# A decoder trunk on one core: the down products of the last two feed-forward steps as one, inside the normalisation, and three of four query latent weight blocks prepared early

## What is computed

```python
def _swiglu(x, w_gate, w_up, w_down):
    return (jax.nn.silu(x @ w_gate) * (x @ w_up)) @ w_down

def _shared_latent(x, pos, wkv_a, kv_norm):
    kv = x @ wkv_a                                    # 1024 -> 256 + 64
    return _rms_norm(kv[..., :256], kv_norm), _rope(kv[..., 256:], pos)

# in each layer, h being the mixer's or the attention's output
x = _layer_norm(ALPHA * x + h, ln_g[l, 0], ln_b[l, 0])
x = _layer_norm(ALPHA * x + _swiglu(x, w_gate[l], w_up[l], w_down[l]), ln_g[l, 1], ln_b[l, 1])
# layer 1 begins with _shared_latent(x, ...) and _rms_norm(x @ wq_a, q_norm)     # 1024 -> 384
```

## Time and profile before

| | us |
|---|---|
| median of 3 runs (lowest, highest) | 2610.28 (2603.63, 2615.92) |
| the profiled execution's own time | 2611.03 |
| its span in the trace | 2609.2 |
| PE busy | 2415.3 |
| DVE busy | 1294.6 |
| ACT busy | 769.7 |
| POOL busy | 347.1 |

### The profile page before, as it was taken

The page is one execution under the profiler, slowest core; times in us unless marked ns, Lnnn a source line. Parts: engine busy times, 40 slices in busy tenths (PEclk is TensorE's granted clock), DMA queues, the critical chain, the costliest instruction groups (busy, mean ns, idle before and its releaser), DMA issues.

```text
span 2609.2 us, 35320 instructions
## 1 busy us (share of the span) xinstructions
PE 2415.3 (93%) x14022; PEld 2198.0 (84%) x14022; DVE 1294.6 (50%) x2467; ACT 769.7 (30%) x1469; POOL 347.1 (13%) x308
## 2 busy tenths in 40 slices
PE   7899999999999768999998888898999999999994
PEld 7799999999999667898987667687999989999993
DVE  4623433333333765677767778643234434433336
ACT  2331111111111233555546556412311111111112
POOL 2400000000000330000006545032000000000006
PEclk9899999999999888999999999899999999999997
DMA  4021111111111031000004444500211111101111
GB/s 158 26 65 49 49 48 35 29 48 48 48 49 41 20 121 44 18 14 5 11 21 158 155 152 152 179 25 25 65 49 49 34 49 49 50 30 36 49 41 65
DMA packets 137082, 153.99 MB, mean 59 GB/s; under 512 B 10256, under 2 KB 114224, under 8 KB 136808
## 3 DMA queue, kind: packets, MB, share of 16 engines
q1 hardware_dynamic: 124656, 110.07, 13.4%
q0 software_dynamic: 12288, 41.95, 5.1%
HBM read 142.24 MB, written 10.32 MB: 58 GB/s over the span
## 4 chain that ended last, share of the span: by engine, by line
PE 80%; DVE 9%; ACT 4%; issue 3%; POOL 2%; DMA 2%; SPq 0%; POOLq 0%; ACTq 0%; DVEq 0%
PE ps L214 23%; PE ps L216 22%; PE ps L215 22%; DVE split L207 4%; ACT split L202 2%; PE ps L2010 2%; PE ps L2045 2%; POOL plain L338 1%; POOL plain L340 1%; PE ps L2025 1%; PE ps L222 1%; PE ps L221 1%; PE ps L2026 1%; PE ps L2032 1%; PE ps L1555 1%
## 5 line engine op out<-in xcount | busy, mean ns | idle before, releaser
L214 PE MATMUL ps<-split 128*128 128x512 f32 (+6 forms) x3632 | 1244.5, 343 | 69.9 <-DVE split L207 23.6
L215 PE MATMUL ps<-split 128*128 128x512 f32 (+6 forms) x3632 | 1229.2, 338 | 0.0
L216 PE MATMUL ps<-split 128*128 128x512 f32 (+6 forms) x3632 | 1228.1, 338 | 0.0
L214 PEld LDWEIGHTS ps<-split 128*128 128x128 f32 x3632 | 694.5, 191 | 120.1 <-DVE split L207 28.9
L216 PEld LDWEIGHTS ps<-split 128*128 128x128 f32 x3632 | 694.8, 191 | 38.0
L215 PEld LDWEIGHTS ps<-split 128*128 128x128 f32 x3632 | 694.8, 191 | 37.1
L202 ACT ACTIVATE split<-plain 128x1024 fp32r<-128x1024 f32 (+8 forms) x446 | 313.3, 738 | 628.7 <-PE ps L222 406.1
L207 DVE TENSOR_TENSOR split<-plain,split 128x1024 fp32r<-128x1024 f32 (+7 forms) x422 | 355.7, 867 | 193.1 <-ACT split L202 190.2
L274 DVE TENSOR_TENSOR plain<-plain,ps 128x512 f32<-128x512 f32 (+2 forms) x396 | 268.6, 685 | 201.9 <-PE ps L216 196.6
L910 DVE TENSOR_TENSOR plain<-plain,ps 128x350 f32<-128x350 f32 (+1 forms) x132 | 68.1, 516 | 574.6 <-ACT plain L866 574.0
L207 DVE TENSOR_TENSOR split<-ps,split 128x512 fp32r<-128x512 f32 (+5 forms) x480 | 247.6, 555 | 153.9 <-ACT split L202 146.4
(11 more groups left out here) (145 smaller groups left out, 1427.1 us busy)
## 6 DMA issues: line engine op xcount, KB each, us to landing
plain<-w_gate SPq DMA_DIRECT2D x44, 512.0 KB, 4.7
plain<-w_up SPq DMA_DIRECT2D x44, 512.0 KB, 4.0
plain<-w_down SPq DMA_DIRECT2D x44, 512.0 KB, 4.4
plain<-x_prompt SPq DMA_DIRECT2D x8, 512.0 KB, 11.2
x_spill<-plain SPq DMA_DIRECT2D x1, 4096.0 KB, 18.6
plain<-wo SPq DMA_DIRECT2D x8, 512.0 KB, 4.9
plain<-x_spill SPq DMA_DIRECT2D x8, 512.0 KB, 7.7
y_prompt<-plain SPq DMA_DIRECT2D x8, 512.0 KB
```

The lines of the kernel that those rows point to most:

```text
L214: pe.matmul(out, still[0], moving[0], start=start, stop=False)
L215: pe.matmul(out, still[0], moving[1], start=False, stop=False)
L216: return pe.matmul(out, still[1], moving[0], start=False, stop=stop)
```

## The change

In both layers, step 10 does no down products of step 9 any more. The normalisation stage's units (`down_last`) sum four chunks, two of step 9 and two of step 10, so that there are ten groups of 18 units instead of eleven. A unit then is 12 matmuls, for the tail 8. The hidden parts of both parities are read; the last two blocks of w_down are split earlier, between the chunks of step 10, into slot 0 of the gate and up buffer (`split_down_last`, `wd_last`), which the first chunk of step 10 has left. PE waits for the hidden part per tile.

In layer 0, blocks 2 and 3 of wkv_a are split at step 9 of the normalisation stage instead of step 3, since block 2 lies where `k.wd` and the hidden parts were. Blocks 4, 5 and 6 of the latent weights are split at units 3, 5 and 7, and only block 7 at unit 9. SP's load of the tables stands behind the last block of wq_a instead of behind that of wkv_a. The places of the eight blocks are a list of offsets now.

```diff
--- before.py
+++ after.py
@@ -155,7 +155,8 @@
         every = {n: rows for n in ("stats", "root", "scale", "normed", "gained", "rows")}
         every.update({n: 2 * tiles + 1 for n in ("turned", "turned_hi", "turned_lo")})
         every.update(gain_in=32, norm_steps=7 * rows + 2, unit_done=2 * rows, unit_taken=2 * rows)
-        ffn = dict(every, unit_done=2 * rows * steps, unit_taken=2 * rows * steps, steps=2 * steps - 2, x_scaled=rows)
+        ffn = dict(every, unit_done=2 * rows * (steps - 1), unit_taken=2 * rows * (steps - 1), steps=2 * steps - 4,
+                   x_scaled=rows)
         ffn.update({"raw_in%d" % i: 2 * 16 * steps for i in range(3)})
         ffn.update({n: 6 * steps for n in ("w_hi", "w_lo")})
         ffn.update({n: 2 * PARTS * steps for n in ("gu_done", "silu", "h_mul")})
@@ -649,6 +650,7 @@
     def __init__(self, k, layer, nt):
         self.k, self.layer, self.nt, self.ph = k, layer, nt, "ffn%d" % layer
         self.steps = k.ff // (2 * P)
+        self.groups = self.steps - 1
         self.x_ph = ("mix", "att")[layer]
 
     def name(self, name):
@@ -752,8 +754,8 @@
 
     def latent_weights(self, eng, step, act):
 
-        if self.layer == 0 and step == 3:
-            for n in range(4):
+        if self.layer == 0 and step in (3, self.k.tiles + 1):
+            for n in ((0, 1) if step == 3 else (2, 3)):
                 latent_split(eng, self.k, n, act)
 
     def split_tile(self, eng, st, i, hi, lo, act):
@@ -771,6 +773,17 @@
         for m in range(2):
             hi, lo = (self.k.wgu[:, slot, m, q].rearrange("p c n -> p (c n)") for q in range(2))
             self.split_tile(eng, st, i + m, hi, lo, act)
+
+    def wd_last(self, q, c):
+
+        return self.k.wgu[:, 0, c, q].rearrange("p c n -> p (c n)")
+
+    def split_down_last(self, eng, act):
+        st = self.steps - 1
+        if act:
+            eng.wait_ge(*self.k.s.at(self.name("gu_done"), PARTS * (2 * st + 1)))
+        for m in range(2):
+            self.split_tile(eng, st, 4 + m, self.wd_last(0, m), self.wd_last(1, m), act)
 
     def split_down(self, eng, st, i, group, act):
         if act and not (isinstance(group, int) and group < 1):
@@ -790,6 +803,8 @@
                 self.split_down(eng, st, 2, st - 1, act)
         elif not last:
             self.split_gate_up(eng, st, 4, 2 * st + 2, 0, act)
+        else:
+            self.split_down_last(eng, act)
 
 
     def gate_up(self, pe, st, slot, p):
@@ -822,8 +837,7 @@
 
             if t == 0:
                 pe.wait_ge(*self.k.s.at(self.name("h_lo"), 2 * (PARTS + 1) * (group + 1)))
-                pe.wait_ge(*self.k.s.at(self.name("w_lo"), 6 * group + 10 if not (isinstance(group, int) and group == self.steps - 1)
-                           else 6 * self.steps))
+                pe.wait_ge(*self.k.s.at(self.name("w_lo"), 6 * group + 10))
             for e in range(2):
                 u = 18 * group + 2 * t + e
                 pe_unit_free(pe, k, self.ph, u)
@@ -838,18 +852,40 @@
                         mm = product_tail(pe, out[0:LO + nt], k.h_tail[:, par, c, 0:LO + nt], w, c == 0, c == 1)
                 mm.then_inc(self.s("unit_done"), 1)
 
+        def down_last(t):
+
+            st = self.steps - 1
+            if t == 0:
+                pe.wait_ge(*self.k.s.at(self.name("w_lo"), 6 * self.steps))
+            p = next(p for p in range(PARTS) if min((t + 1) * P, k.seq) <= self.part(p)[1])
+            pe.wait_ge(*self.k.s.at(self.name("h_lo"), 2 * (PARTS + 1) * st + self.h_count(PARTS + (p if t < k.tiles else 2))))
+            for e in range(2):
+                u = 18 * (self.groups - 1) + 2 * t + e
+                pe_unit_free(pe, k, self.ph, u)
+                out = ps[:, unit_bank(2 * t + e), :]
+                cols = slice(e * BANK, (e + 1) * BANK)
+                for n in range(4):
+                    par, c = (st - 1 + n // 2) % 2, n % 2
+                    w = (k.wd[:, 0, c, cols], k.wd[:, 1, c, cols]) if n < 2 else \
+                        (self.wd_last(0, c)[:, cols], self.wd_last(1, c)[:, cols])
+                    if t < k.tiles:
+                        rows = slice(t * P, (t + 1) * P)
+                        mm = product(pe, out, (k.h[:, par, 0, c, rows], k.h[:, par, 1, c, rows]), w, n == 0, n == 3)
+                    else:
+                        mm = product_tail(pe, out[0:LO + nt], k.h_tail[:, par, c, 0:LO + nt], w, n == 0, n == 3)
+                mm.then_inc(self.s("unit_done"), 1)
+
         def body(st, par):
             for slot in range(2):
                 for p in range(PARTS):
                     if not (isinstance(st, int) and st == 0 and slot == 0 and p < PARTS - 1):
                         self.gate_up(pe, st, slot, p)
-            if isinstance(st, int) and st == 0:
+            if isinstance(st, int) and st in (0, self.steps - 1):
                 return
             for t in range(k.tiles + 1):
                 down(st - 1, 1 - par, t)
 
-        last = self.steps - 1
-        self.steps_of(pe, body, lambda: pe_norm_stage(pe, k, self.ph, nt, lambda t: down(last, last % 2, t),
+        self.steps_of(pe, body, lambda: pe_norm_stage(pe, k, self.ph, nt, down_last,
                                                       self.layer == 0, self.latent_products(pe)))
 
 
@@ -891,7 +927,6 @@
 
         def last():
 
-            self.split_down(act, self.steps - 1, 4, self.steps - 1, True)
             act_norm_stage(act, k, self.ph, nt, self.layer == 0, lambda step: self.latent_weights(act, step, True))
 
         self.steps_of(act, body, last)
@@ -933,8 +968,7 @@
                     dve_add_unit(dve, k, self.ph, 18 * (st - 1) + 2 * t + e, t, e, nt, False, chain)
 
         def last():
-            self.split_down(dve, self.steps - 1, 4, self.steps - 1, False)
-            dve_norm_stage(dve, k, self.ph, nt, self.layer == 0, False, unit0=18 * (self.steps - 1),
+            dve_norm_stage(dve, k, self.ph, nt, self.layer == 0, False, unit0=18 * (self.groups - 1),
                            extra=lambda step: self.latent_weights(dve, step, False))
 
         self.steps_of(dve, body, last)
@@ -982,7 +1016,7 @@
         w, width = (k.wkv_a, k.kv_w) if n < 4 else (k.wq_a[0], k.q_w)
         sp.dma_start(k.lat_raw(n), w.rearrange("(c p) e -> p c e", p=P)[:, 2 * (n % 4):2 * (n % 4) + 2, :])\
           .then_inc(s["lat_raw_in%d" % (n % 4)], 16)
-        if n == 3:
+        if n == 7:
             sp.wait_ge(*s.at("ffn0_rows", k.tiles + 1))
             sp.dma_start(k.rope_rows[:, :, :], k.in_rope_rows.rearrange("p (t c) -> p t c", t=k.tiles + 1))\
               .then_inc(s["lat_tables_in"], 16)
@@ -1017,7 +1051,9 @@
     if act:
         if n == 0:
             eng.wait_ge(*s.at("ffn0_gu_done", 2 * PARTS * k.ffn[0].steps))
-        if n == 5:
+        if n == 2:
+            eng.wait_ge(*s.at("ffn0_unit_done", 18 * k.ffn[0].groups))
+        if n == 7:
             eng.wait_ge(s["lat_unit_done"], k.tiles + 1)
         eng.wait_ge(s["lat_raw_in%d" % (n % 4)], 16 * (n // 4 + 1))
         hi_part(eng, hi, k.lat_raw(n)).then_inc(s["lat_w_hi"], 1)
@@ -1030,7 +1066,7 @@
     s, nt, half = k.s, k.ns + k.nm, k.tiles + 1
     t, w = u % half, latent_width(k, u)
     if u == 0:
-        pe.wait_ge(*s.at("ffn0_unit_taken", 18 * k.ffn[0].steps))
+        pe.wait_ge(*s.at("ffn0_unit_taken", 18 * k.ffn[0].groups))
         pe.wait_ge(s["lat_w_lo"], 4)
     if u == half:
         pe.wait_ge(s["lat_w_lo"], 8)
@@ -1091,8 +1127,7 @@
     for step in range(latent_tasks(k) + 3):
         u = step
         if u == half:
-            for p in range(5, 8):
-                latent_split(act, k, p, True)
+            latent_split(act, k, 7, True)
         if u < latent_tasks(k):
             n = P if u % half < k.tiles else nt
             rms = k.rank if u < half else k.q_w
@@ -1107,8 +1142,8 @@
             act.wait_ge(s["lat_square"], u + 1)
             act.activation(k.lat_root[0:n, u:u + 1], k.lat_ss[0:n, u:u + 1], ACT.Sqrt, bias=k.rms_eps[0:n, 0:1],
                            scale=1.0 / rms).then_inc(s["lat_root"], 1)
-            if u == 4:
-                latent_split(act, k, 4, True)
+            if u in (3, 5, 7):
+                latent_split(act, k, 4 + (u - 3) // 2, True)
         if step >= 3:
             v = step - 3
             act.wait_ge(s["lat_turned"], v + 1)
@@ -1170,12 +1205,11 @@
 
     for step in range(latent_tasks(k) + 4):
         if step == half:
-            for p in range(5, 8):
-                latent_split(dve, k, p, False)
+            latent_split(dve, k, 7, False)
         if step < latent_tasks(k):
             take(step)
-            if step == 4:
-                latent_split(dve, k, 4, False)
+            if step in (3, 5, 7):
+                latent_split(dve, k, 4 + (step - 3) // 2, False)
         if 1 <= step <= latent_tasks(k):
             finish(step - 1)
         if step >= 4:
@@ -1184,7 +1218,7 @@
 
 def latent_pool(pool, k):
 
```

(13 more changed lines are left out.)

## The result

The changed kernel takes 2569.1 us (median of 4, 2564.9 to 2574.1) against 2609.7 us before in the same comparison: a ratio of 0.985, with a 95% interval of 0.983 to 0.986. 2572 was forecast. The profiled execution has a span of 2567.8 us, 41.4 us less than before.

A forecast was written before the change was run, and what follows sets the result against it. Both final stages were taken as bound by DVE's and POOL's row work, with PE waiting. Layer 0's 18.2 us (20.4 less 2.2) and layer 1's 20.4 made 38.6 us, giving 2572 us, range 2559 to 2584.

The forecast's parts named there:

- The down products: Final normalisation stage, both layers: merged products take twice 23.8 us, 47.6, at full clock; DVE's 18 fewer adds cost nothing.
- The pace argument: Final stages: PE needs 5.44 us per tile, 6.3 with transposes, against DVE's 5.17, so PE becomes the bound.
- Step 3's splits: Layer 0's normalisation, latent blocks 0 and 1: low parts take 6.0 us beside POOL, PE waits 3.0, 4.3 charged.
- The second rival: Layer 0: both pairs of low parts miss POOL, cost 1.9 us each, step 3 stalls nothing; 2566 us, 15 in 100.
- (a): Layer 0, from the last unit's end to the last row from POOL: 19.3 us instead of 18.8, +0.5.
- two adds of the tail 1.4: Layer 0 behind the last unit: DVE isn't behind and has two tail adds left, 1.4 us.
- layer 1's gain: Layer 1: POOL ends at 2586.2 instead of 2606.6, a gain of 20.4 us, ends 17 and 22.
- (b): Layer 0, POOL's last row to row 0's output landing, 22.5 us before: wq_a loads go ahead of the tables, -3.8.
- (c): Latent stage, row 0's output landing to PE's restart, 22.75 us before: spread splits hold DVE for ACT, +5.5.
- The transposes' waits in mid stage: Rival, layer 0: the five waits on POOL stay and the clock with them; 2590 us, 12 in 100.
- The half clock: Rival: merged products run at the half level, each 0.2 us more, +83 us, 2655; 3 in 100.
- The stall on row 0's output: Sign, latent stage: the stall is still there, near 12 us, with 27 to 29 us from its end to the restart.

## Why the prediction was right, step by step

The sum was 38.6 us off the profiled execution, and 41.4 came.

- **The down products.** Twice 23.8 us at the full clock was right, in both layers (47.5 in layer 1 by the window), and DVE's missing adds were worth nothing by themselves, as said. The pace argument was tested apart from the wait and holds.
- **Step 3's splits.** 6.0 us for the two low parts, 3.0 of bank wait and 4.3 in all were charged; 5.40, 2.42 and about 3.5 came (the version that moves them). The choice of the upper bound, made on the order of ACT and POOL, was right; the row's median would have been too low. The second rival, that the splits miss POOL, is out: they met it at both places (5.40 and 5.32 us for two). A low part that does miss POOL costs 0.83, less than the 1.9 with which that rival reckoned.
- **(a), from the last unit to POOL's last row:** 19.3 forecast, 20.3 measured. The term that was sized wrong is "two adds of the tail 1.4". Each of the tail's two units takes two adds, and all four of 0.68 were still to come, from 897.58 to 900.38 in layer 0: DVE was still at tile 7's statistics and tile 6's scale when the tail's first unit ended. In the row below, of layer 1, the first tail add starts 0.3 us before PE's last unit ends (2549.1), and ACT gets its scale 5.3 us behind that end, not 4.15. The same term made layer 1's gain 19.5 instead of 20.4.

```profile
2548.80 0.67 DVE L275 TENSOR_TENSOR plain<-plain,ps 8x512 f32<-8x512 f32 x1
...
2554.40 2.42 ACT L329 ACTIVATE plain<-plain 128x1024 f32<-128x1024 f32 x2 [0.92 <-DVE plain L321]
```

- **(b), the queue:** 18.7 forecast, 17.0 measured. The mechanism was right and the size off. The bytes of wq_a gave 3.4 us (the spill lands in 15.2 instead of 18.6), as against 3.8 charged; but the issue of the four loads had held SP for 2.0 us as well, and that wasn't counted. The spill is now issued 1.4 us behind the last row, before it was 3.4. No run moved the load of the tables alone, so these two sizes are read from the traces.

```profile
x_spill<-plain SPq DMA_DIRECT2D x1, 4096.0 KB, 15.2
```

- **(c), the spread splits:** 28.25 forecast, 28.05 measured, and the version with the old places gives 4.7 us back. DVE's timeline of the changed kernel shows what was meant by a split that holds DVE: at unit 5 the take at 943.16 is followed by ACT's square and high part, and the low part starts only 2.1 us later.

```profile
943.16 0.48 DVE L1167 COPY plain<-ps 128x320 f32<-128x320 f32 x1
945.27 0.96 DVE L208 TENSOR_TENSOR split<-plain,split 128x768 fp32r<-128x768 f32 x1 [1.64 <-ACT split L203]
```

- **The rivals.** The transposes' waits in mid stage went; only the last one stayed. The half clock never came in the merged stages (1.00 in both windows).
- **The signs.** Four of those named for the forecast were off. POOL was to be idle for 1 us or more between rows; in layer 1 it is 0.5 to 0.7, which is what 5.44 us of PE less two operations and their gaps leave. The stall on row 0's output was to be near 12 us; ACT waits 7.9, since the output lands in 8.9 us instead of 12.5. The last unit was to end 47 to 52 us after the last gate and up matmul; in layer 0 it is 55.4, and the prediction's own sum had 56.1. POOL's last operation was to end 15 us behind layer 1's last unit; it is 16.1, by the tail's adds. Low parts of 2.5 to 3.0 us, and 28.1 us from the landing to the restart, came as named.
- **Small slips of the sum.** 5.17 less 1.28 for the adds and 1.28 for the low parts is 2.6, not 2.75; five matmuls at 0.2 are 1.0, not 1.1. The low end of the range, 2560, is 2 us below what its two named terms give (8 and 2 off 2572). None of this decides anything.

That the total was met to about 0.1% is partly luck: layer 0 gained 1.6 us more than forecast and layer 1 0.9 less, and the untouched middle added 1.8 of its own spread.

## What to carry to other kernels

Where a stage pairs each product with a round of row work on another engine, compare the two periods: moving matmuls from the stretch before into that stage added no PE time here and stopped the queueing, since PE's period became the longer one. Preparatory work belongs where its engines idle, and that is a matter of which engine bounds that very stretch: here three splits cost 8.2 us more among units bound by DVE than in the idle time of ACT and DVE before them. A small transfer that somebody waits for should be issued ahead of a large one on the same queue, and a sum of a queue has the issue times in it, not the bytes alone.

## What was not expected of the hardware

The clock did not fall at every wait of PE's. After the 2.42 us wait at tile 3 one matmul took 0.50 us and the next were at full speed, in the changed kernel (granted clock 1.00 from 870 to 874 us), while before the change a wait of 2.19 us had been followed by matmuls of 0.63 (0.73 from 905.6 to 912). In the first case PE had been busy without a break for the 25.6 us since the stage began, and before that; in the second it had waited 4.0 us at 888.2, 3.9 at 896.0 and 0.5 at 900.0. No run here varied this alone, so the condition stays open.

```profile
870.14 0.50 PE L215 MATMUL ps<-split 128*128 128x512 f32 x1 [2.42 <-DVE plain L275]
```
